# The order of the double experts, a fifth fixed expert, and the place of the second norm's vectors

## The reference, cut to what matters

```python
x = _layer_norm(DEEPNORM_ALPHA * x + mix, ln1_g, ln1_b)
ffn = _hierarchical_moe(x, rg_w, rg_b, re_w, re_b, e_gate, e_up, e_down)   # 32 experts, 2 per token
x = _layer_norm(DEEPNORM_ALPHA * x + ffn, ln2_g, ln2_b)
return x + jax.nn.sigmoid(x @ ple_gate_w) * (p_i @ ple_proj_w)
```

## Time and profile before

| | |
|---|---|
| median of 3 runs | 718.91 us (718.03 to 720.73) |
| the profiled execution | 722.0 us |
| its span, first to last instruction | 720.2 us |
| TensorE busy | 650.6 us, 90% |
| VectorE / ScalarE / GpSimd busy | 50% / 25% / 23% |
| moved by DMA | 151.21 MB |
| expert stage, first gather to last `down` | 382 to 646 us |

### The profile page before, as it was taken

The page is one execution under the profiler, slowest core; times in us unless marked ns, Lnnn a source line. Parts: engine busy times, 40 slices in busy tenths (PEclk is TensorE's granted clock), DMA queues, the critical chain, the costliest instruction groups (busy, mean ns, idle before and its releaser), DMA issues.

```text
span 720.2 us, 10082 instructions
## 1 busy us (share of the span) xinstructions
PE 650.6 (90%) x3766; PEld 447.7 (62%) x3766; DVE 362.1 (50%) x847; ACT 179.2 (25%) x344; POOL 168.8 (23%) x175
## 2 busy tenths in 40 slices
PE   4999999989989998889957999999999998776997
PEld 3768887767776776768834555555555553433885
DVE  3379998667656568634954112211111111118756
ACT  5175132333323324320211111111111110124311
POOL 7206414010010001162203233333333332111100
PEclk9959999999999999989986999999999999998899
DMA  6402401202200220148685787999999999987003
GB/s 237 191 1 89 147 30 60 116 0 74 103 1 0 85 92 0 60 172 335 252 330 213 272 328 290 408 416 415 414 413 414 413 415 416 418 346 289 24 0 117
DMA packets 30502, 151.21 MB, mean 210 GB/s; under 512 B 7372, under 2 KB 7628, under 8 KB 16496
## 3 DMA queue, kind: packets, MB, share of 16 engines
q1 hardware_dynamic: 24048, 142.08, 50.3%
q0 software_dynamic: 6400, 8.42, 3.3%
HBM read 148.36 MB, written 14.68 MB: 226 GB/s over the span
## 4 chain that ended last, share of the span: by engine, by line
PE 60%; DVE 10%; DMA 6%; SPq 3%; issue 2%; ACT 1%; POOL 1%; DVEq 0%; POOLq 0%; ACTq 0%
PE bank L1990 16%; PE bank L2005 9%; PE bank L1671 7%; PE bank L1672 7%; PE bank L1673 7%; DMA raw<-in_w_exp_dram 4%; SPq L470 3%; PE bank L1751 2%; PE bank L1980 2%; PE bank L1760 2%; PE bank L1772 2%; PE bank L1801 1%; PE bank L1997 1%; PE bank L1792 1%; DVE a_lo L1353 1%
## 5 line engine op out<-in xcount | busy, mean ns | idle before, releaser
L1583 DVE COPY rows_x<-bank 128x128 f32<-128x128 f32 x40 | 11.7, 292 | 195.8 <-PE bank L1997 195.8
L1671 PE MATMUL bank<-w_hi,a_hi 128*128 128x384 f32 (+1 forms) x240 | 92.3, 384 | 3.9 <-POOL w_lo L610 2.8
L1672 PE MATMUL bank<-w_lo,a_hi 128*128 128x384 f32 (+1 forms) x240 | 89.8, 374 | 0.0
L1673 PE MATMUL bank<-w_hi,a_lo 128*128 128x384 f32 (+1 forms) x240 | 89.5, 373 | 0.0
L1671 PE MATMUL bank<-a_hi,w_hi 128*128 128x512 f32 (+1 forms) x176 | 70.4, 400 | 11.4 <-POOL w_lo L603 9.9
L699 POOL DMA_INDIRECT pair_dram<-rows_x,row_put x40 | 40.5, 1013 | 167.0 <-ACT rows_x L953 167.0
L1990 PE MATMUL bank<-raw,rows_x 128*64 128x256 f32 x544 | 65.1, 391 | 6.6 <-DMA raw<-in_w_exp_dram 5.6
L1672 PE MATMUL bank<-a_lo,w_hi 128*128 128x512 f32 (+1 forms) x176 | 69.0, 392 | 0.0
L1673 PE MATMUL bank<-a_hi,w_lo 128*128 128x512 f32 (+1 forms) x176 | 68.8, 391 | 0.0
L1990 PEld LDWEIGHTS bank<-raw,rows_x 128*64 128x64 f32 x544 | 40.4, 141 | 35.3 <-issue 15.0
L1990 PE MATMUL bank<-slots,rows_x 128*64 128x256 f32 x512 | 58.5, 380 | 3.2 <-DMA slots<-in_w_exp_dram 3.2
(11 more groups left out here) (257 smaller groups left out, 1025.6 us busy)
## 6 DMA issues: line engine op xcount, KB each, us to landing
raw<-in_w_exp_dram SPq DMA_DIRECT2D x42, 1024.0 KB, 15.7
slots<-in_w_exp_dram SPq DMA_DIRECT2D x36, 1024.0 KB, 11.9
rows_x<-in_w_exp_dram SPq DMA_DIRECT2D x12, 1024.0 KB, 13.6
raw<-in_w_in_dram SPq DMA_DIRECT2D x19, 512.0 KB, 3.7
raw<-in_w_wide_dram SPq DMA_DIRECT2D x4, 1536.0 KB, 6.7
y<-in_w_exp_dram SPq DMA_DIRECT2D x6, 1024.0 KB
raw<-in_w_out_dram SPq DMA_DIRECT2D x4, 1024.0 KB, 5.9
raw<-pair_dram SPq DMA_DIRECT2D x8, 512.0 KB, 7.2
```

What stands on the lines that cost most here:

```text
L1671: t_.matmul(o, lh, rh, start=first, stop=False)
L1672: t_.matmul(o, lh, rl, start=False, stop=False)
L1673: return t_.matmul(o, ll, rh, start=False, stop=last)
```

## The change

`ORDER` is written anew. Before, ranks 0 to 4 come first and the other double ranks 5, 6 and 7 stand at places 7, 10 and 13; now ranks 0 to 4 come first and ranks 5, 6 and 7 stand at places 12, 18 and 24. A constant `FIX = 5` takes the place of `SLOTS` where fixed experts are meant: expert 4 is fixed, the first table has 10 columns, the second 30. SP issues the three loads of expert 4 before its wait for the sort. The two loads of the second norm's vectors move from behind place 4 to behind the last expert piece.

```diff
-ORDER = [0, 1, 2, 3, 4, 8, 9, 5, 10, 11, 6, 12, 13, 7] + list(range(14, NE))
+FIX = 5
+ORDER = list(range(FIX)) + list(range(8, 15)) + [5] + list(range(15, 20)) + [6] + list(range(20, 25)) + [7] + \
+        list(range(25, NE))
-FIXED = 2 * SLOTS
+FIXED = 2 * FIX
+REST = ITEMS - FIXED
...
                 for s in (2, 3):
                     load(s, s, 2)
+                for q in range(3):
+                    load(4, 4, q)
                 sp.wait_ge(s_rows, 3)
                 before = None
-                for n in range(SLOTS, NE):
+                for n in range(FIX, NE):
                     e = sp.value_load(order[0:1, ORDER[n]:ORDER[n] + 1], min_val=0, max_val=NE - 1)
                     for q in range(2):
-                        if n >= RINGS:
-                            sp.wait_ge(s_gu, 2 * LAST[n - RINGS] + q + 1)
+                        sp.wait_ge(s_gu, 2 * LAST[n - RINGS] + q + 1)
                         load(e, n % RINGS, q)
-                    if n == SLOTS:
-                        sp.dma_start(ln_g, d["ln2_g"].partition_broadcast(P)).then_inc(s_lnw2, 16)
-                        sp.dma_start(ln_b, d["ln2_b"].partition_broadcast(P)).then_inc(s_lnw2, 16)
-                    if n > RINGS:
+                    if n > FIX:
                         sp.wait_ge(s_dn, LAST[n - RINGS - 1] + 1)
-                    if n > SLOTS:
                         load(before, (n - 1) % RINGS, 2)
                     before = e
                 sp.wait_ge(s_dn, LAST[NE - RINGS - 1] + 1)
                 load(before, (NE - 1) % RINGS, 2)
+                sp.dma_start(ln_g, d["ln2_g"].partition_broadcast(P)).then_inc(s_lnw2, 16)
+                sp.dma_start(ln_b, d["ln2_b"].partition_broadcast(P)).then_inc(s_lnw2, 16)
...
-            for e in range(SLOTS):
-                g.memset(sort_base[:, e:e + 1], float(NE - 1 - e + (SLOTS - e) * 2 ** 15)).then_inc(s_rc, 1)
+            for e in range(FIX):
+                g.memset(sort_base[:, e:e + 1], float(NE - 1 - e + (FIX - e) * 2 ** 15)).then_inc(s_rc, 1)
...
             columns(FIXED, ITEMS)
-            values(found, NE)
+            values(found[:, :, 0:REST], REST)
...
-                    tables(TB_FIXED + 3, NE)
+                    tables(TB_FIXED + 3, REST)
```

## The result

The changed kernel takes 723.27 us (median of 15 runs, 718.36 to 725.75) against 719.98 us of the kernel before (15 runs on the same chips, 716.11 to 725.01). The ratio is 1.0051, with a 95% interval of 1.0026 to 1.0076: slower by 3.7 us, between 1.9 and 5.5. The forecast was +3.1 us, 722.0, with a range of 717.0 to 726.0. The difference sits right on the bound of 0.5% that the chances were split at.

What follows compares the result with a forecast made beforehand. The prediction took DMA of expert weights, never free from about 446 us, as the bound. Its terms 0 + 0.3 + 0.4 + 0.1 + 2.3 = 3.1 us on 718.9 gave 722.0 us, range 717.0 to 726.0.

Steps and rivals of the forecast that it cites:

- What bounds the kernel: Expert stage: TensorE sets the pace up to 445 us, DMA is never free from about 446; weight waits cost 13.0 us.
- Part 1: Expert stage: the new order of places gains 0, as the bytes from place 9 on stay the same.
- The +0.3 us for the rows of expert 5: Gathers behind 445 us: expert 5 at a later place makes them carry 29 more rows, 0.12 MB, costing +0.3 us.
- the first wait on place 24: Expert stage: TensorE's first wait for weights comes near 576 us, on place 24, instead of 588.
- Rival (c): Expert stage: double places save TensorE's waits, up to 13.0 us, if buffers bound the last stretch; 709.0 us, chance 0.09.
- Part 3: Tail behind the experts: the vectors' 1.05 MB delay the gate pieces, so the second expert sum starts later, +2.3 us.
- Rival (a): Tail behind the experts: the vectors cost nothing, slipping into a queue that thins out after 640 us; 719.7 us, chance 0.22.
- Part 2: First gather: expert 4's loads ahead of the sort slow it by +0.4 us, between bounds of 0 and +3.7.
- rival (b): First gather: it meets expert 4's weights and takes 7.2 us, costing 3.7 instead of 0.4; 725.3 us, chance 0.15.
- the forecast's sign of 3.5 to 4 us: First gather: taking 3.5 to 4 us would show the forecast right.
- its sign against part 2 (above 5 us): First gather: taking above 5 us would break the forecast's claim for the early loads.
- The table work: Tables ahead of the first gather: 10 columns instead of 8 in the first cost about +0.1 us.

Runs made afterwards that it cites:

- z_light: Kernel before, but from place 10 on only three quarters of each weight piece loaded, so its result is not the reference's; one execution, 699.8 us.
- x_order: Kernel before with only the new order of places (ranks 5, 6, 7 at places 12, 18, 24); ratio 0.9999 to the kernel before.
- x_vectors: Kernel before with only the second norm's two vectors loaded behind the last expert piece; 721.83 against 718.03 us, ratio 1.0054.
- x_warm_after: Changed kernel with the last embedding product computed twice more in TensorE's idle time ahead of the second norm's transposes; ratio 1.0058 to the kernel before.
- x_back: Changed kernel with the second norm's vectors loaded behind the wait for the sort again; ratio 1.0042 to the kernel before.
- x_fifth: Changed kernel with the old order and the vectors back behind the wait for the sort, leaving the fifth fixed expert and its early loads; ratio 1.0052 to the kernel before.
- x_early: Changed kernel with the second norm's two vectors moved ahead of expert 4's early loads; ratio 1.0073 to the kernel before.
- y_three: Kernel before with three fixed experts, single places ahead of the other double ones, vectors ahead of the sort, tables in their own buffer; 712.65 us, ratio 0.9928.

## Why the prediction was right, point by point

**What bounds the kernel** held. z_light removes bytes and the gate/up blocks' waits for weights are gone to the last; DMA was nearly idle ahead of place 9's load in both kernels and full behind it.

**Part 1, the order: 0, measured 0** (x_order, and 193.2 to 194.3 us behind place 9's load with either order). The +0.3 us for the rows of expert 5 is shown by no run; it is smaller than that scatter. The forecast put the first wait on place 24, near 576 us; it came on place 22, at 564, since a place took 194.21 / 22.7 = 8.57 us on average and not the 8.3 that I used. The second wait that it did foresee, for place 24's last piece, cost 3.7 us and not 1 or 2. That made no difference, as the bytes behind decide. Rival (c) falls with x_order.

**Part 3, the vectors: +2.3, measured +2.5 to the second sum**, by the mechanism named: gate pieces behind 1.05 MB, ScalarE's roundings waiting, the sums following. Rival (a) falls with x_vectors. The reason given for taking +2.3 does not hold as it stands: the rows of pieces 1 and 2 show transfers that are still to land, but by the windows DMA's mean share was 0.65 at 644 us and 0.17 at 650, so the queue was not busy to 652 us on all 16 engines. What the sum left out is that the later tail also lengthens TensorE's idle time ahead of the transposes, from 1.9 to 4.5 us. That costs 0.45 us at the transposes, as in x_vectors; and where the kernel before finds its clock up at the gate, the vectors may cost up to 2.8 us more. No run separates this last share.

**Part 2, the early loads: +0.4, measured +1.0 in the changed kernel, +1.35 in x_warm_after, +1.8 in x_back.** This is the term that was mis-sized, and the step is "its rows move from 383.2 on, when at most 0.2 us of weights are left". The end of the weights, 383.4 us, was worked out well, but both times were read off one execution, in which the routing ran at half clock and the gather came 1.3 us late relative to the loads. In x_fifth, whose profile fell in the same case, it was 0.4 us just as forecast. The true answer was between the forecast and rival (b), with (b)'s mechanism; the forecast's sign of 3.5 to 4 us was missed, its sign against part 2 (above 5 us) came in x_back and not in the changed kernel. The Trainium skill ("DMA: Bandwidth & Descriptors", section "Queues, rings and completion order") has each DMA engine take a whole packet from one queue before it turns to the next. That speaks for a cost nearer the upper end; x_early with 7.5 us shows such a cost, but no run here shows an engine's turns. The table work came to less than 0.1 us; 16 more elements at (0.42 - 0.23) / 192 us each are 0.016 us a step, not 0.012, which changes nothing.

**The sum.** 3.1 us was forecast, the ledger has 4.3 and the ratio 3.7 (1.9 to 5.5). Of the ledger's 4.3, 0.4 is scatter of the stage, 2.9 are the vectors and 1.0 the gather. That the total came so near is in part luck: the gather was put too low by 0.6 to 1.4 us, the transposes at nothing, and the rows of expert 5 at 0.3 that no run shows. x_vectors and x_fifth add to more than the changed kernel shows (1.0054 and 1.0052 against 1.0051), 3.9 and 3.7 us against 3.7. The excess of 3.9 us is as large as the half widths of the three intervals taken together (2.8, 2.2 and 1.8 us, root of the squares 3.9, an estimate). x_vectors' interval (1.1 to 6.6 us) holds the 2.9 of its profile, x_fifth's (1.6 to 5.9) holds the dearest gather, 1.8, and not the 1.0 of the changed kernel. So the parts are only measured to within 2 or 3 us by their ratios, their sizes rest on the profiles, and why x_fifth is as slow as that stays open.

## What to carry to other kernels

When transfers are the bound of a stage, find the last moment at which the queue is idle: nothing that is done to the queue ahead of it helps, and reordering work behind it only moves the waits. To gain, move that moment forward (give the early places less work per byte loaded) or take bytes out from behind it. And before two profiles are compared, look where else they differ: here the clock and one wait moved single stretches by 1 to 3 us from one execution to the next, as much as the change did. And bytes that nothing reads yet are not free wherever they are put: issue 1 MB where the queue is idle, not ahead of a small gather and not ahead of the loads that the next stage begins with.

## What the runs showed of the hardware that was not expected

- A small indirect gather (38 tokens of 4 KB, 0.16 MB) pays for weights in flight: 3.3 to 3.6 us on an idle queue (nine profiles), 3.9 when the weights end some 1.4 us behind its issue (x_fifth), 4.5 to 5.3 when they end 2 to 3.5 us behind it (after, x_warm_after, x_back), 7.5 us when 1.05 MB more of them are queued (x_early).
- TensorE's granted clock takes different courses between its two levels in the same program, in three places: the second half of the routing (19.6 or 18.2 us from store to gather), item 0's gate/up block (4.4 to 6.0 us, and 58.1 to 58.6 or 59.4 to 59.7 us from the transposes to place 9's load) and the gate's first matmuls (51.4 or 54.2 us to the end, 53.0 in two). Together that is some 5 us, an estimate from these three differences, while the executions of the kernel before spread over 9 (716.1 to 725.0).
- An SP issue stood for 6.6 us with a full queue in front, against 0.43 us in y_three. The first gate pieces were issued 1.6 us later than before, counted from item 39's second half, but the last one, which the sums wait for, was issued 3.2 us ahead of that half in both kernels.
